# A two-block transformer kernel on one core: two of its norms add their squares on VectorE and sum over the partitions with one product

## The reference

```python
def rms_norm(x, gain=None):
    xf = x.astype(jnp.float32)
    y = xf * lax.rsqrt(jnp.mean(xf * xf, axis=-1, keepdims=True) + EPS)
    ...
def modulate(h, shift, scale):
    return h * (1.0 + scale) + shift
...
    for l in range(DEPTH_2):
        ...
        x = x + 0.5 * mx[2] * swiglu_2(modulate(rms_norm(x), mx[0], mx[1]), *ffn1)
        xc = xc + 0.5 * mc[2] * swiglu_2(modulate(rms_norm(xc), mc[0], mc[1]), *ffn1)
```

## Time and profile before

| what | value |
|---|---|
| median of 3 runs | 2590.28 us (2585.96 to 2595.58) |
| profiled execution | 2593.13 us, its span 2591.3 us |
| TensorE busy | 2494.1 us (96%) |
| VectorE busy | 1335.6 us (52%) |
| ScalarE busy | 1035.0 us (40%) |
| mean granted clock of TensorE | 0.985 |

### The profile page before, as it was taken

How to read it: one execution, slowest core, us unless ns; L and a number is a source line. 1 busy time by engine, 2 the same in 40 slices (tenths; PEclk the granted TensorE clock), 3 DMA queues, 4 the chain that set the end, 5 groups by cost and what they waited for, 6 DMA issues and landing times. The chain is left out here.

```text
span 2591.3 us, 37219 instructions
## 1 busy us (share of the span) xinstructions
PE 2494.1 (96%) x15710; PEld 2161.8 (83%) x15710; DVE 1335.6 (52%) x2198; ACT 1035.0 (40%) x1660; POOL 0.2 (0%) x4
## 2 busy tenths in 40 slices
PE   7999999989999999999888999999999998988999
PEld 6998789978998888888567888888888887878999
DVE  6657454655554333456886433335333337846553
ACT  5534444444433223146562322213222226744443
POOL 0000000000000000000000000000000000000000
PEclk9999999999999999999998999999999999999999
DMA  8986733488862333335102333333333336502564
GB/s 307 306 266 215 244 122 99 139 311 303 313 227 87 94 96 97 98 114 187 58 1 66 90 98 98 98 98 90 98 98 97 95 93 171 186 18 66 175 183 147
DMA packets 146727, 372.28 MB, mean 144 GB/s; under 512 B 20330, under 2 KB 67074, under 8 KB 146562
## 3 DMA queue, kind: packets, MB, share of 16 engines
q1 hardware_dynamic: 146274, 369.59, 44.4%
q10 hardware_dynamic: 288, 0.31, 0.1%
HBM read 368.71 MB, written 1.15 MB: 143 GB/s over the span
## 5 line engine op out<-in xcount | busy, mean ns | idle before, releaser
L298 DVE TENSOR_TENSOR weights_lo<-weights_raw,weights_hi 128x1024 fp32r<-128x1024 f32 (+2 forms) x547 | 657.4, 1212 | 485.0 <-ACT weights_hi L292 482.9
L350 PE MATMUL psum<-normed_hi,weights_hi 128*128 128x256 f32 (+2 forms) x2664 | 884.1, 332 | 22.6 <-DVE normed_lo L629 6.5
L350 PE MATMUL psum<-normed_lo,weights_hi 128*128 128x256 f32 (+2 forms) x2664 | 869.9, 327 | 0.0
L350 PE MATMUL psum<-normed_hi,weights_lo 128*128 128x256 f32 (+2 forms) x2664 | 869.3, 326 | 0.0
L292 ACT CAST weights_hi<-weights_raw 128x1024 fp32r<-128x1024 f32 (+2 forms) x547 | 562.7, 1035 | 374.1 <-DMA weights_raw<-in_w_down 254.3
L350 PEld LDWEIGHTS psum<-normed_hi,weights_hi 128*128 128x128 f32 (+1 forms) x2664 | 512.0, 192 | 86.0 <-issue 35.1
L350 PEld LDWEIGHTS psum<-normed_lo,weights_hi 128*128 128x128 f32 (+1 forms) x2664 | 513.2, 193 | 41.5 <-issue 1.2
L350 PEld LDWEIGHTS psum<-normed_hi,weights_lo 128*128 128x128 f32 (+1 forms) x2664 | 512.9, 193 | 40.7
L350 PE MATMUL psum<-hidden_hi,weights_hi 128*128 128x512 f32 (+1 forms) x594 | 217.6, 366 | 0.0
L350 PE MATMUL psum<-hidden_hi,weights_lo 128*128 128x512 f32 (+1 forms) x594 | 217.1, 365 | 0.0
L350 PE MATMUL psum<-hidden_lo,weights_hi 128*128 128x512 f32 (+1 forms) x594 | 217.0, 365 | 0.0
(11 more groups left out here) (264 smaller groups left out, 2724.1 us busy)
## 6 DMA issues: line engine op xcount, KB each, us to landing
weights_raw<-in_w_gu SPq DMA_DIRECT2D x220, 512.0 KB, 3.6
weights_raw<-in_w_down SPq DMA_DIRECT2D x110, 512.0 KB, 3.6
arena<-in_w_mod SPq DMA_DIRECT2D x72, 512.0 KB, 7.1
weights_raw<-in_w_x SPq DMA_DIRECT2D x24, 512.0 KB, 7.4
resid<-in_w_mod SPq DMA_DIRECT2D x24, 512.0 KB, 7.6
normed_raw<-in_w_mod SPq DMA_DIRECT2D x24, 512.0 KB, 6.9
under_normed_hi<-in_w_mod SPq DMA_DIRECT2D x24, 512.0 KB, 7.2
weights_raw<-in_w_qk SPq DMA_DIRECT2D x24, 512.0 KB, 3.7
```

The source lines that it names most:

```text
L298: ve.tensor_tensor(w_lo[:, c % RING, a], w_raw[:, c % RING, a], w_hi[:, c % RING, a].bitcast(F32), ALU.subtract).then_inc(lo_ready, 1)
L350: last = te.matmul(out, a, b, start=start and n == 0, stop=stop and n == 2)
```

## The change

The two norms with eight products now do what the first norm does: VectorE adds the eight squares in seven additions into `squares[:, 0]`, and TensorE makes one product of that. All three norms with squares of their own signal the end of the additions by a semaphore of its own, `squares_added`, and the first norm no longer takes a place in the count of `squares_summed`. The last line of the difference takes out a value that nothing reads.

```diff
--- before.py
+++ after.py
@@ -243,6 +243,7 @@
             sem(n + "_landed") for n in ("columns", "ones", "constants", "rel_table", "context"))
         tokens_in = [sem(f"tokens_landed_{n}") for n in range(2)]
         bias_in, bias_rows = sem("bias_landed"), sem("bias_rows_ready")
+        squares_added = sem("norm_squares_added")
         squares_summed, norm_sum, norm_av, norm_vv, normed_ready = (
             sem("norm_" + n) for n in ("squares_summed", "sum_ready", "scalar_done", "vector_done", "tile_ready"))
         hid_hi, hid_ready = sem("hidden_hi_ready"), sem("hidden_lo_ready")
@@ -259,7 +260,7 @@
 
         counts = {"bias": 48, "normed": 0, "sums": 0, "norm_sum": 0,
                   "norm_av": 0, "norm_vv": 0, "hidden": 0, "heads": 0, "turns": 0, "turned_hi": 0, "pairs": 0, "joint": 0,
-                  "single": 0, "sub": 0, "evac_act": 0, "evac_dve": 0, "merged": 0, "halves": 0, "norms": 0}
+                  "single": 0, "sub": 0, "evac_act": 0, "evac_dve": 0, "merged": 0, "halves": 0, "norms": 0, "added": 0}
 
         def take(name, n):
             counts[name] += n
@@ -536,13 +537,14 @@
 
             def __init__(self, a, gain, shift, into=None, squares_at=None, summed=None, first_chunk=False):
                 self.a, self.gain, self.shift, self.first_chunk = a, gain, shift, first_chunk
+                self.added0 = take("added", 1) if squares_at is not None else None
                 self.in_place, self.squares_at = into is not None, squares_at
                 self.sides = range(a.start // S, a.stop // S)
                 n_sq = KD if squares_at is not None else 0
                 self.sum0, self.vv0 = take("norm_sum", 1), take("norm_vv", 1 + KD)
                 self.av0 = take("norm_av", n_sq + 1 + (0 if self.in_place else KD))
                 self.rms0 = self.av0 + n_sq
-                self.summed = take("sums", 1) + 1 if first_chunk else summed or counts["sums"]
+                self.summed = summed or counts["sums"]
                 self.bank_read = counts["norms"]
                 counts["norms"] = self.vv0 + 1
                 self.normed0 = None if self.in_place else take("normed", KD)
@@ -555,14 +557,11 @@
                 if self.bank_read:
                     pe.wait_ge(norm_vv, self.bank_read)
                 w = self.a.stop - self.a.start
-                if self.squares_at is None or self.first_chunk:
+                if self.squares_at is None:
                     pe.wait_ge(squares_summed, self.summed)
-                    last = te.matmul(psum[:, NORM_BANK, 0:w], ones, squares[:, 0, self.a], start=True, stop=True)
                 else:
-                    for k in range(KD):
-                        pe.wait_ge(norm_av, self.av0 + k + 1)
-                        last = te.matmul(psum[:, NORM_BANK, 0:w], ones, self.squares_at[:, k, :],
-                                         start=(k == 0), stop=(k == KD - 1))
+                    pe.wait_ge(squares_added, self.added0 + 1)
+                last = te.matmul(psum[:, NORM_BANK, 0:w], ones, squares[:, 0, self.a], start=True, stop=True)
                 last.then_inc(norm_sum, 1)
 
             def scalar(self, act, step, i):
@@ -593,7 +592,7 @@
 
             def vector(self, dve, step, i):
                 w = self.a.stop - self.a.start
-                if self.first_chunk:
+                if self.squares_at is not None:
                     total = squares[:, 0, self.a]
                     for k in range(1, KD):
                         dve.wait_ge(norm_av, self.av0 + k + 1)
@@ -601,7 +600,7 @@
                                                 self.squares_at[:, k, :], ALU.add)
                         if k < KD - 1:
                             step(last)
-                    last.then_inc(squares_summed, 1)
+                    last.then_inc(squares_added, 1)
                 dve.wait_ge(norm_sum, self.sum0 + 1)
                 ve.tensor_scalar(rstd[:, self.a], psum[:, NORM_BANK, 0:w], 1.0 / D, EPS, ALU.mult, ALU.add
                                  ).then_inc(norm_vv, 1)
@@ -1619,7 +1618,6 @@
                 self.s, self.turned = s, turned
                 self.base = take("pairs", len(units))
                 self.stat = small[:, 128:128 + 16].rearrange("p (b n) -> p b n", b=4)
-                self.joint0 = take("joint", 0)
                 joint, single = take("joint", 0), take("single", 0)
                 for u in units:
                     if u.lam is not None:
```

## The result

| | median | runs |
|---|---|---|
| before | 2589.76 us (2584.45 to 2595.58) | 10 |
| changed kernel | 2598.24 us (2595.86 to 2600.06) | 10 |

The ratio is 1.003, with a 95% interval of 1.0018 to 1.0042: 4.7 to 10.9 us slower, and within 0.5%. The forecast was "within 0.5%" at +4.4 us; the time lies in its range, on the slow side of the sum.

What follows compares the result with a forecast made beforehand. TensorE, busy 96%, was taken as the bound, waiting for the norm's chain at the second block's first norm. Terms 2.2 + 0.2 + 2.0 + 0 = +4.4 us on the 2590.28 median gave 2594.7 us, range 2587 to 2600.

Steps and rivals of the forecast that it cites:

- Place and sign: At both norms, TensorE passes removed become idle time for dependent additions: slower by 4.4 us, busy time lower without shorter span.
- Second block's first norm, +2.2: Two splits, seven additions, then one product at the halved clock: sum read and stream restarted 2.2 us later.
- the other price of +1.6: Second block's first norm: delay if the clock is full at the product, read after 0.63 us instead of 1.23.
- Context's norm, +0.2 for the chain: Additions from 631.23, product at 634.47, modulation's products at 634.92 instead of 634.69: 0.2 us later at full clock.
- Context's norm, +2.0 for the clock: TensorE idles about 4.4 us, then restarts at the halved clock: 2.0 us lost, bounds 0 and 2.8.
- the bound of 2.8: Upper bound of the context's norm clock loss, from 26 passes in 6.00 us from 1422.60 at the halved clock.
- The splits queued behind, 0: VectorE's splits after the context's norm come up to 0.9 us later; cost taken as 0, bounds 0 and 0.7.
- Passes count in full: Rival: additions keep up with ScalarE's squares, so 6.3 us of TensorE passes go, 2584.0 us; chance 0.08.
- a full clock at both products: Rival: the clock stays full at both restarts, then only +1.8 us, 2592.1; chance 0.12.
- The halved clock lasting long behind the restarts: Rival: clock stays halved long behind both norms, slower by over 0.5% from some 14 us each; chance 0.05.

Runs made afterwards that it cites:

- both_sums: Changed kernel, with TensorE also making the eight products over the squares at both norms, their result overwritten by the one product; 2594.62 us, ratio 1.0007 to before.
- x_only: Against before, only the second block's first norm adds its squares on VectorE, the context's norm keeps its eight products; 2594.03 us, ratio 1.0006.
- after_again: The changed kernel once more, nothing altered, beside before on the same chip; 2597.72 us against 2591.49, ratio 1.0028.
- ctx_only: Against before, only the context's norm adds its squares on VectorE, the second block's first norm keeps eight products; 2595.90 us against 2592.79, ratio 1.0015.
- before_again: The kernel before, nothing altered, profiled a second time; a single run, 2591.9 us.
- the last kernel: Against before: context's norm with additions, cut in three steps; second block's first norm one chunk earlier with eight products; 2584.00 us against 2591.82, ratio 0.9969.
- x_earlier: Against before, only the second block's first norm moved one chunk earlier in the order, eight products kept; 2589.49 us against 2591.49, ratio 0.9997.

## Why the prediction was right, and where its sum was short

**Place and sign: right.** TensorE's passes were traded for idle time, at both norms; its busy time fell without a shorter span.

**Second block's first norm, +2.2: right.** Measured 8.97 - 6.82 = +2.15 in the changed kernel, by the steps as written: splits, additions 0.46 apart, product at the halved clock, reading after 1.23 us. Where the clock was full at the product, in `both_sums`, it was 1.57, the other price of +1.6; in `x_only`, where it fell while the product ran, 1.76. The first passes behind run at 0.50 as before and cost nothing more; up to the pass at 793.26 the delay is 1.8.

**Context's norm, +0.2 for the chain: right.** From the last pass to the product it took 632.87 - 628.21 = 4.66 us, where the prediction has 634.47 - 629.92 = 4.55.

**Context's norm, +2.0 for the clock: the right mechanism, its size too small in two profiles of three.** In the changed kernel's profile the product lasted 1.13 us instead of 0.45, the modulation's products 3.57 instead of 1.86, and the stream from 637.57 to 638.80 ran at 0.50, which at 0.47 us lost per us is 0.6: 0.7 + 1.7 + 0.6 = 3.0, above the bound of 2.8. In `after_again` the clock was back as the stream began, 2.4; in `ctx_only` the product was at the full clock, 0.2 + 1.6 = 1.8. The value taken lay between two rows of before; the row with the longer stretch, 2.8, was nearer to what this place gives. It has a wait of 4.4 us, longer than any in before away from the start (3.3), and behind it work that takes nearly twice as long at 0.50: 3.57 / 1.86 = 1.92 times for the modulation's products. The Trainium skill, "TensorE: Matmul & The Clock Gate", section "HAM oscillation — how this bites in real kernels", reckons the loss as half of the throttled time. Here it is a little less: 1.71 of 3.57 us, or 0.48, for these products, and 0.47 by the prediction's reckoning from the earlier trace rows.

**The splits queued behind, 0: right.** TensorE waits for none in the 141.63 us behind the context's norm.

**The sum.** Between the same passes (the table above) the two places give 3.3 + 1.8 = 5.1 us in the changed kernel's first profile and 2.7 + 1.8 = 4.5 in `after_again`: near the +4.4, and inside the bounds of +1.8 to +5.9. The medians gave +8.5 (4.7 to 10.9) and +6.2 (4.1 to 10.4 by its ratio). The intervals hold 5.1, but both medians lie above it, by 3.4 and 1.1 us. The two profiles cannot say where this goes: they are of the fastest runs of their kernels (2595.86 and 2592.63 us), and outside of the two places they took 2.4 and 5.1 us less than the first profile of before, from which `before_again` differs there by 0.9. So the loss of some 5 us at the two places is shown, and what the medians add to it stays open. The prediction has no term for it; that 2598.24 still lies below 2600 it owes to the margin for the spread in its range.

**Rivals.** "Passes count in full" fell: 6.3 us of passes went and the time rose. Of the kernels with additions at both norms, a full clock at both products was seen only in `both_sums`, where TensorE was given work. The halved clock lasting long behind the restarts was not seen: in the first profile the stream was back at 1.00 by 638.80 and by 792.40.

## What to carry to other kernels

Moving work off the busiest engine gained nothing here while that engine had nothing else to do meanwhile: 16 passes and seven dependent additions take about the same time, so the exchange turned work into waiting, and the waiting lowered the clock for the work behind it. Ask first where the engine will stand while the other one does the work, and place the consumer later, as the last kernel does; then look at what the freed engine runs into next, here the banks. And follow a gain to the end of the program: that of `x_earlier` was there at its place and lost at another. In the order of an engine, an instruction that a chain needs must not stand behind work that nobody waits for yet, neither its first part nor the reading at its end.

## What was not expected of the hardware

- Making TensorE work more made the changed kernel's norm faster: with 16 passes whose result is thrown away, the context's norm took 7.07 us instead of 9.36, and the clock stayed at 1.00.
- Additions that depend on one another start 0.46 us apart at a duration of 0.42, while VectorE's independent splits of 1.22 us run two in 2.35, so that the second starts about 0.09 ahead of the first one's end. The eight tiles of the first block's last norm (line 615), each 128x256 and independent of the others, take 3.25 at a duration of 0.48, so they start 0.40 apart and overlap by 0.08. An estimate from these: waiting for the result before costs about 0.12 us an instruction here, 0.7 us in six steps.
- A norm whose code and place were the same ran at 0.50 in one execution and at 1.00 in another, 26 against 52 passes in 6.00 us.
